# A halo tile moved ahead of the last chunk, three slot pairs of the up projection in front, and earlier weight loads, in a decoder block on eight cores

## What is computed

```
mod = silu(c) @ ada_w + ada_b                    # shift1 scale1 gate1 shift2 scale2 gate2
h = rms_norm(x, norm1_g) * (1 + scale1) + shift1
q, k, v, p, g_attn, g_pool = split(h @ w_in)     # w_in 1024 x 4096
attn = moba_attention(rms(q), rms(k), v)         # 8 heads x 64, own block of 256 keys and the top 3 earlier ones
pool = multiscale_pool(p) @ pool_w * pool_scale  # trailing windows 2, 4, 8, 16
merged = sigmoid(g_attn) * (attn @ w_branch_attn) + sigmoid(g_pool) * (pool @ w_branch_pool)
x = x + gate1 * (merged @ w_out)
h2 = rms_norm(x, norm2_g) * (1 + scale2) + shift2
u = causal_dwconv3(h2 @ w_up)                    # w_up 1024 x 5632
x = x + gate2 * ((silu(u_g) * u_v) @ w_down)     # w_down 2816 x 1024
```

## Time and profile before

| | us |
|---|---|
| median of 3 runs | 2089.19 |
| the three runs | 1950.83, 2089.19, 2097.91 |
| the profiled execution, device time | 1955.46 |
| its span on the slowest core (core 6) | 1953.9 |
| spans of the eight cores | 1932.5 to 1953.9 |
| PE busy | 1739.9 (89%), 13700 matmuls |
| DVE, ACT, POOL busy | 1093.0, 1073.2, 657.6 |
| mean granted TensorE clock, core 6 | 0.957 |

### The profile page before, as it was taken

How to read it: one execution, slowest core, us unless ns; L and a number is a source line. 1 busy time by engine, 2 the same in 40 slices (tenths; PEclk the granted TensorE clock), 3 DMA queues, 4 the chain that set the end, 5 groups by cost and what they waited for, 6 DMA issues and landing times.

```text
span 1953.9 us, 39700 instructions; the slowest of 8 cores (1932.5 to 1953.9 us)
## 1 busy us (share of the span) xinstructions
PE 1739.9 (89%) x13700; PEld 1191.3 (61%) x13700; DVE 1093.0 (56%) x1486; ACT 1073.2 (55%) x1395; POOL 657.6 (34%) x609
## 2 busy tenths in 40 slices
PE   7668999989987989796989999988976999999998
PEld 3335555555554767675767777754435888887443
DVE  1555555556556564635363554426765888887222
ACT  1435545445535878676778988953334666665000
POOL 1778777677672000000000000005774444442000
PEclk9889999999998989898989999989997999999999
DMA  9793454534455131414132120514749534340332
GB/s 254 160 178 119 123 143 104 143 100 124 114 127 126 47 89 30 114 48 121 51 92 49 20 58 2 87 37 138 193 140 175 49 34 45 34 42 9 108 116 94
DMA packets 245741, 187.48 MB, mean 96 GB/s; under 512 B 158293, under 2 KB 211925, under 8 KB 244457
## 3 DMA queue, kind: packets, MB, share of 16 engines
q1 hardware_dynamic: 186378, 154.93, 29.0%
q0 software_dynamic: 59168, 30.02, 12.7%
HBM read 170.77 MB, written 44.12 MB: 110 GB/s over the span
## 4 chain that ended last, share of the span: by engine, by line
PE 72%; POOL 6%; issue 5%; ACT 5%; DVE 5%; DMA 4%; SPq 2%; DVEq 0%; POOLq 0%; ACTq 0%
PE psum L387 70%; ACT arena L395 4%; POOL arena L403 3%; SPq L400 2%; POOL arena L441 2%; PE psum L391 2%; DVE arena L403 2%; DMA arena<-ada_w 2%; DMA arena<-w_in 1%; ACT arena L419 1%; DMA arena<-xw 1%; DVE arena L414 1%; POOL arena L439 1%; DVE psum L403 1%; DVE arena L615 1%
## 5 line engine op out<-in xcount | busy, mean ns | idle before, releaser
L387 PE MATMUL psum<-arena 96*128 96x256 bf16 (+7 forms) x12572 | 1674.9, 291 | 154.3 <-ACT arena L395 71.3
L387 PEld LDWEIGHTS psum<-arena 128*128 128x128 bf16 (+3 forms) x12572 | 1122.6, 100 | 687.9 <-issue 265.7
L395 ACT ACTIVATE arena<-psum 128x1024 bf16<-128x1024 f32 (+2 forms) x731 | 637.1, 960 | 356.4 <-PE psum L387 263.9
L403 POOL TENSOR_TENSOR arena<-arena 128x1024 bf16<-128x1024 f32 (+2 forms) x211 | 346.1, 1647 | 310.9 <-ACT arena L395 148.2
L414 DVE SCALAR_TENSOR_TENSOR arena<-psum,arena 128x512 f32<-128x512 f32 (+1 forms) x354 | 266.2, 753 | 86.1 <-PE psum L387 60.7
L403 DVE TENSOR_TENSOR arena<-psum,arena 128x512 f32<-128x512 f32 (+5 forms) x245 | 151.2, 635 | 269.4 <-PE psum L387 146.5
L414 DVE SCALAR_TENSOR_TENSOR arena<-arena 128x1024 f32<-128x1024 f32 (+3 forms) x137 | 208.7, 1529 | 74.2 <-DMA arena<-ada_w 32.0
L395 ACT ACTIVATE arena<-psum,arena 128x512 f32<-128x512 f32 (+4 forms) x220 | 162.4, 738 | 141.0 <-PE psum L387 139.4
L400 POOL DMA_DIRECT2D arena<-wba x1 | 0.8, 771 | 612.1 <-PE psum L387 612.1
L395 ACT ACTIVATE arena<-arena 128x512 bf16<-128x512 f32 (+3 forms) x174 | 144.4, 830 | 88.0 <-DVE arena L403 49.7
L441 POOL TENSOR_TENSOR arena<-arena 128x8 f32<-128x8 f32 (+1 forms) x148 | 186.6, 1264 | 15.8 <-POOL arena L439 0.7
(11 more groups left out here) (24 smaller groups left out, 147.3 us busy)
## 6 DMA issues: line engine op xcount, KB each, us to landing
arena<-xw SPq DMA_DIRECT2D x80, 512.0 KB, 4.2
arena<-ada_w SPq DMA_DIRECT2D x32, 512.0 KB, 4.9
arena<-wup POOLq DMA_DIRECT2D x44, 256.0 KB, 5.0
arena<-ada_w SPq DMA_DIRECT2D x8, 1024.0 KB, 11.4
arena<-w_in POOLq DMA_DIRECT2D x8, 1024.0 KB, 18.1
VS<-arena SPq DMA_DIRECT2D x32, 256.0 KB, 3.8
KS<-arena SPq DMA_DIRECT2D x32, 256.0 KB, 4.2
SGS<-arena SPq DMA_DIRECT2D x8, 1024.0 KB, 6.5
```

The lines of the kernel that those rows point to most:

```text
L387: P.op('tensor', lambda e: e.matmul(out, lhsT=lhsT, rhs=rhs, start=start, stop=stop), R, W, dur=d, mode=(rk(lhsT.shape[0]), rk(fs(lhsT)), ...
L395: P.op('scalar', lambda e: e.activation(out=out, in_=in_, func=func, **kw), R, W, dur=edur('scalar', fs(in_)) + (0.1 if 'accum_out' in kw ...
L403: P.op(eng, lambda e: e.tensor_tensor(out=out, in0=in0, in1=in1, op=op), R, W, dur=edur(eng, fs(out)))
```

## The change

Three edits. The six `w_own` loads take as their predecessor the operation kept in `g1k`: for position 0 the one that makes `G1rep`, afterwards the last of the `stageB` one position earlier. In the out stage all of `hq`, then out_b(11), then out_a(16) come ahead of out_a(12); the last chunk is then only its four tiles, and the order at the end is out_a(15), out_b(14), out_b(15). In the up projection the groups 0 to 2 of slots 0 to 2 come first, then group 3 of slots 0, 1, 2, then slot 3 on as before; `wup_load(3)` still follows `up(0, 3)`. `mT` 0 to 3 lie at 26.5 to 42.5 KB, 4 to 16 at 42.5 to 94.5 KB, 17 to 21 at 6.5 to 26.5 KB.

```diff
--- before.py
+++ after.py
@@ -554,7 +554,10 @@
         P.op('scalar', lambda e: e.mul(gqcol, gqcol, 0.125), ['gqcol'], ['gqcol'])
         TT('vector', gqcol, gqcol, gkcol, ALU.mult, ['gqcol', 'gkcol'], ['gqcol'])
         CP('scalar', shift1rep, psum[:, 0:1024], [('ps', 0), ('ps', 1)], ['shift1'])
+        g1k = [None]
         STT(G1rep, psum[:, 1024:2048], 1.0, g1r, ALU.add, ALU.mult, [('ps', 2), ('ps', 3), 'g1r'], ['G1rep'])
+        g1k[0] = P.last
+
         def w_own(i, after):
             if i == 0:
                 CDMA(Wqp[:, :, 0:512], win_v[:, :, 0:512], [('Wqp', 0)], cast=True, after=after)
@@ -894,7 +897,8 @@
             xload(pos + 3)
             stageB(pos, order[pos])
             if pos % 2 == 0 and pos < 12:
-                w_own(pos // 2, P.last)
+                w_own(pos // 2, g1k[0])
+            g1k[0] = P.last
             done = -1
             if pos >= 1:
                 wt = order[pos - 1]
@@ -1282,6 +1286,11 @@
         outb = []
         for ci in range(4):
             pq = pool_parts(ci + 2) if ci + 2 < 4 else []
+            if ci == 3:
+                while hq:
+                    hq.pop(0)()
+                outb.pop(0)()
+                outb.append(out_a(16))
             for tl in range(4):
                 outb.append(out_a(4 * ci + tl))
                 if ci < 3:
@@ -1290,18 +1299,15 @@
                     for _ in range(2):
                         if pq:
                             pq.pop(0)()
-                elif hq:
-                    for _ in range(3):
-                        if hq:
-                            hq.pop(0)()
                 if len(outb) >= 2:
                     outb.pop(0)()
-        outb.append(out_a(16))
         while outb:
             outb.pop(0)()
 
-        TM = Alloc(6.5, 94.5)
-        mT = [TM([2048], BF16, 'mT%d' % i) for i in range(22)]
+        TM0 = Alloc(26.5, 42.5)
+        TM1 = Alloc(42.5, 94.5)
+        TM2 = Alloc(6.5, 26.5)
+        mT = [(TM0 if i < 4 else TM1 if i < 17 else TM2)([2048], BF16, 'mT%d' % i) for i in range(22)]
         T4x = Alloc(178, 184)
         T4y = Alloc(124.5, 129)
         T4 = Alloc(161.5, 178)
@@ -1356,7 +1362,11 @@
         for fp in range(3):
             wup_load(fp)
         for fp in range(22):
-            for sp in range(4):
+            if fp == 0:
+                for f_ in range(3):
+                    for sp in range(3):
+                        up(f_, sp)
+            for sp in range(3 if fp < 3 else 0, 4):
                 up(fp, sp)
             if fp + 3 < 22:
                 wup_load(fp + 3)
```

## The result

The change made the kernel slower by half a per cent: 1969.35 us, median of 7 runs (1964.24 to 2122.13), against 1954.58 us for the kernel before, run beside it. The ratio is 1.0056, 95% interval 1.0035 to 1.0077, some 11 us. The prediction was 14.3 us faster, 1941 us. The result lies within the 2% that count as no change and inside the range of 1925 to 2090, but outside the forecast's own 1933 to 1949: the sign is wrong. The profiled execution has a span of 1963.4 us on its slowest core, core 7.

What follows compares the result with a forecast made beforehand. Bound: the moment the up projection gets going, plus fixed TensorE work. Out stage and up projection -14.3, slot 3 load +1.0, `w_in` loads -1.0, sum -14.3 us from 1955.5: 1941 us, range 1925 to 2090.

Steps and rivals of the forecast that it cites:

- What bounds the kernel: The end is when the up projection gets going plus fixed work; TensorE is nearly idle from 1470 to 1484 us.
- The halo block: Halo branches ahead of the last chunk: two bare rounds of serial gate loads, 14.0 us, bounds 7 and 21.
- The halo tile: Halo tile ahead of tile 12: 3.6 us of products, its VectorE work falling into slack; moved, not added.
- Tiles 12 to 15: Last chunk's four tiles at VectorE's 4.3 us each: 17.2 us, at most 20.
- Six units forward: Six up projection units run during tile 15's last chain, 10.5 us of products; bounds 0 and 12.1.
- cold start: Low clock over the first 32 up products costs 2.5 us before the change; counted as gone after it.
- The load of slot 3: Up weight load with only two pairs, 7.0 us, before its use: costs 1 us, 8 if cover is gone.
- The `w_in` loads: First stage: six loads one tile earlier end a GpSimd wait; gain 1 us, bounds 5.5 gain and 21.6 loss.
- Rival A: Up projection: no products come forward, the 10.5 us fall away, gain 3.8 us, 1952 us; chance 0.15.
- Rival B: First stage: earlier `w_in` loads double the `xw` waits, +21.6 us, 1964 us, slower than before; chance 0.12.
- Rival C: Halo block fully bare and cold: 21 us of loads, 7.2 of products, +10.6 us, 1952 us; chance 0.13.
- Rival D: More is hidden: halo block 7 us, last chain filled, first stage gaining 5.5 us; 1928 us; chance 0.10.

Runs made afterwards that it cites:

- e2: The changed kernel with the `w_in` loads as in the kernel before; ratio 1.0037 to the kernel before.
- e10: e2 with the halo's gates loaded by one DMA and its branches beside chunk 2, the halo tile still ahead of tile 12; ratio 0.9975.
- e5: e2 with the halo's gates loaded by one early DMA in place of 16 small loads; ratio 1.0025.
- e11: e10 with the `wup` loads of slots 1 and 2 held behind the shifts of tiles 14 and 15; ratio 0.9989.
- e17: e13 with the shift of the halo tile and of tiles 12 to 15 on VectorE in place of GpSimd; ratio 0.9963.
- e14: Kernel before with the halo's gates loaded once and its branches beside chunk 2, the halo tile last as before; no ratio, mean span +3.0 us.
- e13: e11 with the silu of the first three up pairs held behind tile 15's shift; ratio 0.9959.
- e3: Kernel before with the halo tile ahead of the last chunk alone, old up order and old places of `mT`; ratio 1.0044.
- e7: Kernel before with only the first `w_in` load issued early, behind `G1rep`, the other five as before; ratio 0.9986.
- e8: Kernel before with only `w_in` loads 2 to 6 given the change's predecessors, the first as before; ratio 0.9977.
- e1: Kernel before with the change's new predecessors of the `w_in` loads alone; ratio 1.0026.
- e16: e1 run once more, beside other kernels; ratio 1.0021.

## Why the prediction was wrong

- *What bounds the kernel* held. The hole ahead of the up projection was the place, and the halo's chain behind tile 15 did go: the tail is 12.9 us shorter.
- *The halo block, 14.0 us.* The step from tile 11 to 12 was to last 14.0 + 3.6 + 4.3 = 21.9 us and lasted 26.8 (26.1 in e2). The block itself was priced too high: hiding it gave 10.3 us (e10). Nor is it what the text said: serial gate loads alone are 3.5 us (e5), and the text passed over the four `wup` issues (3.60 us) ahead of one of its last adds in GpSimd's list. What outgrew the sum are the other two terms: the halo tile with the `wup` issues beside it, 8.5 us for 3.6 (e10), and tile 12's own turn, 7.3 us as before for 4.3.
- *The halo tile: "It is moved, not added", "into slack of the tiles"* is the step that failed most clearly as an argument. 7.1 us stay when its branches are hidden and the issues are out of the way (e11), against 3.6 of products. Its shift takes 2.33 us on GpSimd and stands ahead of tile 12's root; with the shift on VectorE 1.8 us of it go (e17). It also takes its turn in the two buffers `tmp3`. Before, the same work stood behind tile 15, at 6.2 us. So the move gains nothing by itself; what it gains is the up products that it lets go forward.
- *Tiles 12 to 15, 4 x 4.3 us* is the term that was mis-sized most, by 11.4 us: three steps took 24.3, not 12.9. A sum of one engine's work was taken for the pace, though the kernel before, too, took 22.9 for them; the loop from scaling through the shift to the next scaling gives 5.9 even with nothing beside it (e14), 17.7 for three. Most of the rest is the step 14 to 15, which took 11.9. On core 7, 3.8 us of it lie between the halves of tile 15's root, with the early pair's multiply waiting for silu and its table load; holding these back gave 1.5 us of the step (e13).
- *Six units forward, 10.5 us* was right as a count: 104 products before the end of the last copy, 96 forecast. But the full pace is not there at the copy. From 1500 to 1517 us, 89 products take 17 us; at 0.109 us each they would take 9.7. These 7.3 us on core 7, for clock (granted 0.80) and stops, are of the size of the 6.3 that the mean tail lacks; the text had cancelled the cold start (2.5 us) altogether. That the units need the new order was wrong: 72 products pass in the old one, for a tail as short (e3).
- *The load of slot 3, 1 us:* no load holds up TensorE behind 1517 on core 7; it is hidden.
- *The `w_in` loads, "move forward by one tile each"* is false for five of six on core 0. The operation kept is the store of V at every odd position. Forecast -1; +1.7 and +4.2 in two measurements, -2.5 where the store is not waited for.
- *Rival A* (nothing comes forward) is out by the products at 1489.86. *Rival B* is out: the `xw` waits fell on core 6 from 21.6 us to 12.4, and on every other core too. Its premise holds, though: on core 6 before, an `xw` load lands in 10.2 us beside the `w_in` loads and in 3.7 between 200 and 400 us, where none is under way. *Rival C* was nearest: a bare block and a low clock behind it; but it had placed all of its 28.2 us in loads and products, and would still have given 1952. *Rival D* is out. That the sign turned was covered by no rival at the out stage, where most of it arose: B had it at the first stage, by another mechanism.

What stays open: why the early first load and the late other loads each cost nothing and together cost some us (e7, e8 against e1 and e16), and where in the kernel that time goes; and how the 7.3 us behind the last copy divide between the clock and the stops, which no run took apart.

## What to carry to other kernels

A block of small work that is moved brings all the places that it takes in in-order lists: look up what stands in each list ahead of its last operation, and what of the next tile stands behind it. In these traces a tile of few rows costs the time of a full one on VectorE and GpSimd, so it has no slack to go into where those two set the pace; and the pace of tiles is the longest loop through the engines' lists and the buffers that they share, not the largest engine's sum. "After the last operation" in a builder may be a DMA: then the wait is for its landing.

## What was unexpected of the hardware

GpSimd's shift and VectorE's `TENSOR_TENSOR` shut each other out. Undisturbed the shift takes 2.35 us and the add 1.22. On core 7 after, the add that starts at 1483.87, inside the shift of 1483.23, takes 2.79; at 1450.24 in the rows of e14 the shift starts inside the add of 1449.95 and takes 3.13. Each grows by about the time for which the other still had to run (1.57 against 1.71, 0.78 against 0.93). The Trainium skill, "SBUF — State Buffer", section "Who interferes with whom", says that a VectorE instruction with two SBUF inputs contends with a GpSimd instruction that reads SBUF, and that the order of issue decides which of them blocks. The add has two such inputs, both orders are seen here, and the traces agree. VectorE's passes with one input in PSUM were not held up: two took 1.60 us from 1482.35 on, beside the same shift, and two took 1.61 at 1497.78 with no shift beside them. It is a part of why a busy GpSimd makes VectorE's 4.3 us a tile unreachable.
